# Hybrid decoder block on one core: the split weight tiles moved to four different byte rests in SBUF

## What is computed

```python
h = rmsnorm(x, norm_mix_g)
z = h @ w_in + b_in                      # 1024 x 7456 columns
(ga, gb, gc, fq, fk, fv, ff, cb, cc, cx, nq, ...) = split(z)
y_a = fox_attention(fq, fk, fv, ff) @ w_br_a
y_b = (cb * causal_dwconv(cc * cx)) @ w_br_b
y_c = nsa_attention(nq, ...) @ w_br_c
mix = sigmoid(ga) * y_a + sigmoid(gb) * y_b + sigmoid(gc) * y_c
x = x + mix @ w_o
u, v = split(rmsnorm(x, norm_ffn_g) @ w_up)   # 1024 x 5632
x = x + (silu(causal_dwconv(u)) * v) @ w_down # 2816 x 1024
return rmsnorm(x, norm_final_g)
```

## Time and profile before

| what | value |
|---|---|
| median of 3 runs | 911.8 us (911.68 to 911.94) |
| profiled execution, its own time | 911.65 us |
| its span, first to last instruction | 909.9 us |
| granted TensorE clock, mean over the span | 0.999 of 2.4 GHz |
| PE busy | 894.8 us, 4360 matmuls |
| PEld busy | 745.9 us, 4360 loads |
| DVE, ACT, POOL busy | 503.8, 376.4, 383.6 us |
| HBM traffic | 86.14 MB read, 4.21 MB written |

### The profile page before, as it was taken

One profiled execution on the slowest core, in us unless ns is written; L12 is line 12 of the kernel. 1 busy time (PEld: TensorE's weight loads), 2 busy tenths in 40 slices (PEclk: granted clock), 3 DMA queues, 4 the chain that ended last, 5 costly groups with the idle time before them and its releaser, 6 DMA issues.

```text
span 909.9 us, 13487 instructions
## 1 busy us (share of the span) xinstructions
PE 894.8 (98%) x4360; PEld 745.9 (82%) x4360; DVE 503.8 (55%) x983; ACT 376.4 (41%) x650; POOL 383.6 (42%) x201
## 2 busy tenths in 40 slices
PE   6999999999999999999999999999999999999997
PEld 5888888888888888888887787888888888888885
DVE  4326564648575855756657887666666666400004
ACT  6435354444553553454443444333333333311125
POOL 4454435443324333323234574544444444444441
PEclk9999999999999999999999999999999999999999
DMA  6344342422222322212246434444453333322232
GB/s 189 95 129 116 82 119 76 124 73 71 69 70 70 93 48 82 74 50 74 64 106 150 115 93 116 115 115 117 127 151 113 92 92 104 126 94 93 93 116 92
DMA packets 178930, 90.75 MB, mean 100 GB/s; under 512 B 54463, under 2 KB 169549, under 8 KB 178901
## 3 DMA queue, kind: packets, MB, share of 16 engines
q1 hardware_dynamic: 177813, 90.08, 35.7%
q10 hardware_dynamic: 1088, 0.30, 0.1%
HBM read 86.14 MB, written 4.21 MB: 99 GB/s over the span
## 4 chain that ended last, share of the span: by engine, by line
PE 94%; DVE 2%; ACT 1%; DMA 1%; issue 1%; POOL 0%; SPq 0%; ACTq 0%
PE z_bank L686 24%; PE z_bank L688 24%; PE z_bank L687 24%; PE s_bank L686 3%; PE s_bank L688 3%; PE s_bank L687 3%; PE s_bank L751 3%; PE s_bank L723 3%; PE s_bank L771 1%; PE s_bank L770 1%; PE o_bank L771 1%; PE o_bank L770 1%; DMA x_in<-in_x 1%; PE o_bank L688 1%; PE o_bank L686 1%
## 5 line engine op out<-in xcount | busy, mean ns | idle before, releaser
L587 POOL TENSOR_TENSOR w_lo<-raw,w_hi 128x1024 fp32r<-128x1024 f32 (+1 forms) x144 | 346.8, 2408 | 506.3 <-ACT w_hi L991 421.7
L686 PE MATMUL z_bank<-h_hi,w_hi 128*128 128x512 f32 x768 | 302.3, 394 | 0.1
L688 PE MATMUL z_bank<-h_hi,w_lo 128*128 128x512 f32 x768 | 299.2, 390 | 0.0
L687 PE MATMUL z_bank<-h_lo,w_hi 128*128 128x512 f32 x768 | 299.0, 389 | 0.0
L991 ACT ACTIVATE w_hi<-raw 128x1024 fp32r<-128x1024 f32 x116 | 122.3, 1054 | 173.7 <-PE z_bank L688 173.6
L686 PEld LDWEIGHTS z_bank<-h_hi,w_hi 128*128 128x128 f32 x768 | 144.2, 188 | 31.2 <-issue 0.8
L688 PEld LDWEIGHTS z_bank<-h_hi,w_lo 128*128 128x128 f32 x768 | 144.2, 188 | 30.6
L687 PEld LDWEIGHTS z_bank<-h_lo,w_hi 128*128 128x128 f32 x768 | 144.3, 188 | 28.9 <-issue 0.2
L1616 DVE SCALAR_TENSOR_TENSOR u_c<-u_t,cols,u_c 128x512 f32<-128x512 f32 x44 | 65.7, 1494 | 25.4 <-ACT u_c L1219 22.3
L1000 ACT ACTIVATE p_f<-p_f,neg_mx 128x128 f32<-128x128 f32 (+1 forms) x96 | 52.7, 551 | 41.6 <-DVE neg_mx L1476 27.5
L1631 DVE TENSOR_TENSOR y_out<-s_bank,x_t 128x512 f32<-128x512 f32 x5 | 3.4, 689 | 106.6 <-PE s_bank L688 106.6
(11 more groups left out here) (327 smaller groups left out, 1293.7 us busy)
## 6 DMA issues: line engine op xcount, KB each, us to landing
raw<-in_w_in SPq DMA_DIRECT2D x112, 256.0 KB, 3.2
raw<-in_w_up SPq DMA_DIRECT2D x88, 256.0 KB, 3.2
raw<-in_w_down SPq DMA_DIRECT2D x42, 256.0 KB, 2.9
raw<-in_w_o SPq DMA_DIRECT2D x16, 256.0 KB, 3.3
x_in<-in_x SPq DMA_DIRECT2D x4, 512.0 KB, 5.3
f_bias<-cum_scratch SPq DMA_DIRECT2D x4, 512.0 KB, 4.7
raw<-in_w_br_a SPq DMA_DIRECT2D x8, 256.0 KB, 3.1
raw<-in_w_br_b SPq DMA_DIRECT2D x8, 256.0 KB, 3.4
```

What stands on the lines that cost most here:

```text
L587: pool.tensor_tensor(w_lo[:, slot, 0:wide], raw[:, slot, 0:wide], w_hi[:, slot, 0:wide].bitcast(F), ALU.subtract) \
L686: pe.matmul(out, w[0], r[0], start=first, stop=False)
L687: pe.matmul(out, w[0], r[1], start=False, stop=False)
L688: return pe.matmul(out, w[1], r[0], start=False, stop=last)
```

## The change

Where `w_hi` and `w_lo` were one tile each with two slots, each slot is now a tile of its own, and unused tiles of 32, 32, 96, 32 and 64 bytes stand before the four and behind them. The addresses become 9376 (`w_hi0`, rest 160), 13504 (`w_hi1`, rest 192), 17696 (`w_lo0`, rest 32) and 21824 (`w_lo1`, rest 64). The fillers add up to 256 bytes, so that every later tile moves up by 256 and keeps its rest; `raw` stays where it was. All uses are rewritten from `w_hi[:, slot, ...]` to `w_hi[slot][:, ...]`. No instruction is added, removed or moved.

```diff
         raw = sb("raw", [P128, 2, CH])
-        w_hi = sb("w_hi", [P128, 2, CH], R)
-        w_lo = sb("w_lo", [P128, 2, CH], R)
+        w_hi, w_lo = [], []
+        for name, to in (("w_hi", w_hi), ("w_lo", w_lo)):
+            for slot in range(2):
+                sb(f"{name}_pad{slot}", [P128, (24 if name == "w_lo" and slot == 0 else 8)])
+                to.append(sb(f"{name}{slot}", [P128, CH], R))
+        sb("w_end_pad", [P128, 16])
...
-                return w_hi[:, slot, o:o + P128], w_lo[:, slot, o:o + P128]
+                return w_hi[slot][:, o:o + P128], w_lo[slot][:, o:o + P128]
...
-                        mm = down(j, t, h, w_hi[:, n % 2, :], w_lo[:, n % 2, :], j == 0, False)
+                        mm = down(j, t, h, w_hi[n % 2], w_lo[n % 2], j == 0, False)
...
-                act.activation(w_hi[:, slot, 0:wide], raw[:, slot, 0:wide], ACT.Copy).then_inc(hi_split, 1)
+                act.activation(w_hi[slot][:, 0:wide], raw[:, slot, 0:wide], ACT.Copy).then_inc(hi_split, 1)
```

More of the change, by code:

```diff
@@ L586, in split_lo @@
                 pool.wait_ge(hi_split, n + 1)
-                pool.tensor_tensor(w_lo[:, slot, 0:wide], raw[:, slot, 0:wide], w_hi[:, slot, 0:wide].bitcast(F), ALU.subtract) \
+                pool.tensor_tensor(w_lo[slot][:, 0:wide], raw[:, slot, 0:wide], w_hi[slot][:, 0:wide].bitcast(F), ALU.subtract) \
                     .then_inc(lo_split, 1)
@@ L805, in _ @@
                     o = V2_W * (k - k0)
-                    w = [p[:, n % 2, o:o + V2_W] for p in (w_hi, w_lo)]
+                    w = [p[n % 2][:, o:o + V2_W] for p in (w_hi, w_lo)]
                     for t in range(QT):
@@ L817, in _ @@
                     k = 2 * (n - N_V2) + kk
-                    w = [p[:, n % 2, BR_W * kk:BR_W * kk + BR_W] for p in (w_hi, w_lo)]
+                    w = [p[n % 2][:, BR_W * kk:BR_W * kk + BR_W] for p in (w_hi, w_lo)]
                     for t in range(QT):
@@ L970, in _ @@
                 for h in range(2):
-                    down(FT - 2, t, h, w_hi[:, n % 2, :], w_lo[:, n % 2, :], False, False)
+                    down(FT - 2, t, h, w_hi[n % 2], w_lo[n % 2], False, False)
                     down(FT - 1, t, h, last_hi, last_lo, False, True).then_inc(down_done, 1)
@@ L990, in split_hi_in_loop @@
                 act.wait_ge(tile_done, tiles)
-                act.activation(w_hi[:, slot, :], raw[:, slot, :], ACT.Copy).then_inc(hi_split, 1)
+                act.activation(w_hi[slot][:, :], raw[:, slot, :], ACT.Copy).then_inc(hi_split, 1)
             def evac_hi(dst, src, done, bias=0.0):
```

## The result

The changed kernel takes 927.6 us (median of 4 runs, 926.44 to 928.09) against 911.9 us before (4 runs): the ratio is 1.0172, with a 95% interval of 1.0159 to 1.0184. The forecast was 911.8 us with a range up to 918.5; the change costs 15.7 us, and none of its bounds on the slower side reached that far.

The account below looks back on a forecast made before the run. The prediction took the kernel to be bound by PE, matmul count times distance between starts; its three terms were each taken as nothing, so the forecast stayed at the earlier median, 911.8 us, with a range of 903 to 918.5 us.

Parts of the forecast that it names:

- What bounds the kernel: Whole kernel: time is the number of matmuls times the distance between their starts on PE, 0.2267 us each in both projections.
- Term 2: 2784 matmuls with stationary weights: new rests cost nothing; bounds 4.5 us each way, at the very most 37 us gained.
- Term 1: 696 matmuls with moving weights: nothing, as the middle of 1.6 ns either way, 1.1 us gained or lost.
- equal rests are the good case: Every matmul on weights: unequal rests cost 1.6 ns on each of 3480, 5.6 us slower, 917.4 us; chance 0.26.
- the loads and the stream collide at equal rests: The "faster" rival, every matmul on weights: different rests remove part of 13.3 ns, 2.6 ns or 9 us, 902.8 us; chance 0.36.
- Term 3: ACT and POOL splits writing the weight tiles: address cost stays under 1.7 us of cover in the loop; nothing taken.

Follow-up runs that it names:

- c288_mix: Changed kernel with slot 0 weights at rest 160, slot 1 at 128, and only 288 of each 512 columns computed in the down projection; 886.1 us.
- raw160: Changed kernel with the four weight tiles back at rest 128 and only `raw` moved to rest 160; 911.9 us beside 911.9 of before.

## Why the prediction was wrong

**What bounds the kernel** was right: PE at the distance of its starts, with little else on the path, and the 15.7 us are more of that distance. One reading was off without consequence: the up projection does not end at 722 us. By the starts it runs from 543 to 784 us and the down projection from there on, so both stretches of the earlier trace rows begin in the up projection; the two timelines do lie in the stages that they are said to be in.

**Term 2 failed**, "weights stationary (2784 matmuls) ... I take nothing". It was mis-sized: the runs show 5.2 to 5.8 ns in the up projection, 5.2 us for that stage alone, and all but some 3 us of the 15.7 is in stages where weights are stationary. The witness was the transposes of `lg_t` and `p_f`. I called it weak and still took its nothing; they are the same after the change (0.11 us each), as their own rests didn't move; those of `lg_t` load only 32 columns each, and neither series says anything of float32r matmuls of 512 columns. No row of before had such a matmul at unequal rests, so nothing but a bound was to be had from it, and a bound of 1.6 ns was not one.

**Term 1** took nothing as the middle of 1.6 ns either way; measured are 3.7 ns (slot 1) and 6.2 ns (slot 0) in the down projection. The V2 rows were read rightly, and c288_mix gave the same 133.3 and 131.7 ns again. The mistake was to carry the price of 288 columns over to 512 as if it were one of the start of a matmul. With the weights at 160 and the activations at 128 it is 1.6 ns at 288 columns, nothing at 384 and 6.5 ns at 512.

**The rival "equal rests are the good case"** was the right one: sign, place (every matmul on weights) and the reading of V2 behind it. Its price, 1.6 ns on 3480 matmuls or 5.6 us, was a third of the 15.7 us, and as the range's upper end hung on it, the range missed. The size could not be had from the rows of before; the direction could. It had 0.26, the least of the three directions, though it rested on the only row about float32r and rests, while the "faster" rival rested on an unexplained surplus.

**The rival "the loads and the stream collide at equal rests"** fell twice: no D is faster than 0, and halving or quartering the loads did not bring back any of the 13.3 ns over 512 columns.

**Term 3** held: writers and `raw` don't matter (raw160), POOL's 28 ns a split stayed under cover.

**The pages.** D changes the pace of TensorE's matmuls by up to 7.9 ns in 226.7, with nothing but TensorE's own operands involved. The page "SBUF — State Buffer" of the Trainium skill (section "SBUF: two separate sides") says that PE never waits on anyone; by that rule, as the prediction worked it out, no rest would change anything. Here the measurement decides. What is left at equal rests, 226.7 ns, is over the 216 ns that "TensorE: Matmul & The Clock Gate" (section "Back-to-back issue gap") gives by its formula for 512 columns, without naming a type; no run here brought it down.

**What stays open.** What inside the chip keeps step at D = 0 isn't shown, nor which pair it is that counts: while one matmul streams, the stationary operand of the next is loaded, and no run here tells its own pair from that one. The repeating patterns, the loss of the even pace with shorter loads and the missing price at 384 columns suggest that the delay of one matmul depends on where the one before it left the two reads; that is argued, not shown. That equal rests are good wherever they lie was tried at 128 and at 160 alone. Widths under 512 were tried at a single unequal rest each, besides V2's. It wasn't tried whether the other pairs (scores, P x V) would gain or lose by rests of their own.

## What to carry to other kernels

Before padding or splitting tiles that TensorE reads, look at the byte offset modulo 256 of both operands of the hot matmul, and keep them equal: here that was worth 4 to 6 ns of 227 on each float32r matmul of 512 columns, 1.7% of the kernel, and 8 bytes were enough to lose it. At 384 columns nothing was lost, so measure for other widths. Compare starts, not lengths, 24 matmuls apart. And where the trace has the disputed effect in one shape only, take its sign, but don't take its size for another shape: bound it by the whole surplus in both directions.

## What was unexpected

- The two operands' distance modulo 256 sets the pace, and their own place doesn't, as far as tried: all at 160 is as fast as all at 128 (226.7 ns), one of them off by 8 bytes gives 232.0 to 233.4 ns.
- The price hangs on the width (weights at 160, activations at 128): 1.6 ns at 288 columns (133.3 against 131.7), nothing at 384 (173.3 in both), 6.5 ns at 512 (233.3 against 226.9).
- Loading fewer stationary columns made matmuls slower at equal rests: 226.7 ns with 128, 230.0 with 64, 231.3 with 32.
- Parts don't add up: 17.0 us for the high tiles, 15.7 for the low ones, 15.7 for both.
